# Experts with few rows multiplied in plain fp32 on the two column halves of TensorE, and a new order around gathers, pairs and splits

## The chip, the cores and the metric

The kernel runs on one core of a Trainium2 chip. The metric is the device time of one execution in microseconds (us); three executions of the kernel before took 3588.44 to 3592.20 us, with a median of 3590.94 us.

## What is computed

One layer of a streaming encoder on 1152 tokens of 2048 numbers (1024 of a prompt, 8 x 16 of running streams): a projection, a gated convolution and differential attention, an output projection, then a mixture of experts and a last norm. The change lies in the mixture of experts:

```
lg = hf @ w_rg + b_rg                       # 4 groups of experts, the best one is taken
le_g = (hf @ w_re + b_re)[that group]       # 8 experts in it, the best two are taken
xs = hf[tok_s]                              # tokens in the order of their experts
gate, up = split(ragged_dot(xs, w_ei, sizes))          # w_ei: 32 x 2048 x 1024
ys = ragged_dot(silu(gate) * up, w_eo, sizes)          # w_eo: 32 x 512 x 2048
y = zeros.at[tok_s].add(ys * w_s)
```

Everything is fp32. There are 2304 rows (two per token) over 32 experts. Counted with the reference on its own inputs, experts 0 to 31 get 93, 74, 55, 185, 49, 149, 43, 88, 22, 15, 12, 18, 13, 28, 27, 11, 44, 16, 29, 205, 118, 23, 86, 17, 68, 190, 228, 61, 34, 179, 14 and 110 rows: 19 experts have at most 64, seven have 65 to 128 (0, 1, 7, 20, 22, 24, 31), six have more (3, 5, 19, 25, 26, 29). The eleven experts 8 to 18 are all among the 19.

## The kernel before, in words

`phase_experts` (L1495) works through **groups**, each one expert with up to 256 rows, so here 32 groups, one per expert. A group has one tile of 128 rows, or two (a **pair**), and every tile costs the same however many of its rows are real. First the routing is planned: VectorE (DVE) finds for each row its place, 18 indirect transfers write a table of slots (L1653), and a small plan says for each group its expert and how many pairs lie before it (`group_expert`, `group_pairs`).

For a group, 12 **units** of 1 MB are loaded by the SP queue (`load_unit`, L1485): units 0 to 7 are pieces of `w_ei` (two blocks of 128 rows x 1024), units 8 to 11 are column blocks of `w_eo`. They land in six buffers, `expert_raw`. TensorE multiplies here in a fast format (fp32r) that rounds its operands, so each operand is used as a rounded part and a remainder: ScalarE (ACT) writes the rounded part of a unit, `e_w_hi` (`split_hi`, L1887 to L1891), DVE the remainder, `e_w_lo` (`split_lo`, L1976 to L1979), into four buffers each. The remainder's end frees the raw buffer (`lo_done`), which the next load waits for (L1600). Three products, hi by hi, lo by hi and hi by lo, then make one fp32 product (L1805 into the four PSUM banks `e_gu`, L1782 into `e_y_ps`).

The rows of a group are gathered from HBM by GpSimd's queue (L1640) into `e_x`, turned by TensorE against the identity (L1736, `turn_rows`), and kept as `e_xT_hi` by ACT (L1896) and `e_xT_lo` by DVE (L1984). After the eight units of `w_ei`, ACT computes silu (L1928), DVE multiplies by the other half (L2117), TensorE turns the result (L1769), ACT and DVE keep it as two parts (L1933, L2122), and the four units of `w_eo` follow. In between TensorE turns the next group's rows. ACT copies each output block to `e_y` (L1965), and GpSimd scatters it to `expert_rows` (L1711); the scatter's landing frees `e_y` (`y_free`).

Where the next group is a pair, its second tile is turned in a step of its own at the end of `up_and_first` of the group in front (L1852 to L1860), and kept by ACT and DVE (L1951, L2140), before that group's last three output blocks. In a pair each unit is used for both tiles before the next unit.

Each engine runs its own loop of 40 possible groups, each inside `If(g < count)` (L1566), and chooses between code for one and for two tiles (`by_size`, L1576).

Of the kernel before, what the change touches and what calls it, by code (L numbers as in the profile page):

```python
# [1481 lines left out]
UIN, UOUT = KT // 2, D // 512  # L1482

def load_unit(c, eng, raw, raw_loaded, expert, u):  # L1485

    r = u % RAW
    if u < UIN:
        w = c.io.w_ei.rearrange("e (u a p) n -> e u p a n", a=2, p=P)[ds(expert, 1), u, :, :, :].rearrange("e p a n -> (e p) a n")
    else:  # L1490
        w = c.io.w_eo.rearrange("e (k p) (b n) -> e b p k n", p=P, n=512)[ds(expert, 1), u - UIN, :, :, :].rearrange("e p k n -> (e p) k n")
    eng.dma_start(raw[:, r, :].rearrange("p (a n) -> p a n", a=w.shape[1]), w).then_inc(raw_loaded[r], 16)

def phase_experts(c, raw, raw_loaded, x_back, w_hi, w_lo, rows_back, rows_loaded):  # L1495
# [14 lines left out]
    with ExitStack() as mem:  # L1510
# [5 lines left out]
        pos, rows = sb("e_pos", [P, NP], U32), sb("e_rows", [P, NP, 4], I32)  # L1516
        empty = sb("e_empty", [P, 2 * SLOT_GROUPS, 4], I32)
# [3 lines left out]
        with ExitStack() as once:  # L1521
# [16 lines left out]
            expert_col, paired_col = first("r_expert_col", [P, 1]), first("r_paired_col", [P, 1])  # L1538
# [4 lines left out]
        sg, act_rows = sb("e_sg", [P, 2, DE]), sb("e_act", [P, 2, DE])  # L1543
# [22 lines left out]
        def groups(eng, count, body):  # L1566
# [4 lines left out]

        def pairs(eng, g):

            return eng.value_load(c.group_pairs[0:1, ds(g, 1)], min_val=0, max_val=MAXG)

        def by_size(eng, before, after, part):  # L1576

            with eng.If(before < after):
                part(2)
            with eng.If(before == after):  # L1580
                part(1)
# [12 lines left out]
        with nc.Block() as block:  # L1594

            @block.sync
            def _(sp):
# [20 lines left out]
                groups(sp, count, body)  # L1618
# [19 lines left out]
            def _(pool):  # L1638
# [4 lines left out]
                def gather(g, before, after):  # L1643
# [4 lines left out]
                    gather_tile(0)  # L1648
                    with pool.If(before < after):
                        gather_tile(1)  # L1650
# [12 lines left out]
                pool.memset(empty[:], 0).then_inc(consts, 1)  # L1663
# [7 lines left out]
                pool.memset(empty[:, :, 0:2], NO_ROW).then_inc(consts, 1)  # L1671
                pool.wait_ge(consts, 14)
                pool.dma_start(io.slots.rearrange("(p t) f -> p (t f)", p=P), empty[:].rearrange("p t f -> p (t f)")).then_inc(emptied, 16)
                pool.wait_ge(emptied, 16)
# [5 lines left out]
                p0, p1, p2 = (pairs(pool, g) for g in range(3))  # L1680
# [3 lines left out]
                gather_tile(0)  # L1684
                with pool.If(p0 < p1):
                    gather_tile(1)
# [4 lines left out]
                pool.dma_start(table[:, 2:6, :], slot_tiles[:, 2:6, :]).then_inc(next_loaded, 16)  # L1691
                pool.dma_start(table[:, 6:, :], slot_tiles[:, 6:, :]).then_inc(table_loaded, 16)
                pool.wait_ge(next_loaded, 16)
                pool.wait_ge(x_turned, 4 * p1 + 4)
                gather(1, p1, p2)

                def body(g):
                    here, nx, nx2, nx3 = (pairs(pool, g + i) for i in range(4))
                    pool.wait_ge(table_loaded, 16)
                    pool.wait_ge(x_turned, 4 * (g + nx2 + 2))  # L1700
                    gather(g + 2, nx2, nx3)
# [5 lines left out]
                    def scatter(n):  # L1707
                        pool.wait_ge(y_kept, 4 * (g + here + n) + 2)
                        c.hold(pool)
                        for r in range(n):  # L1710
# [4 lines left out]
                    by_size(pool, here, nx, scatter)  # L1715
# [3 lines left out]
                groups(pool, count, body)  # L1719
                all_pairs = pairs(pool, MAXG)  # L1720
                pool.wait_ge(y_stored, 16 * (count + all_pairs))
                pool.wait_ge(x_loaded, 16 * (count + all_pairs + 2))

            @block.tensor
            def _(pe):
# [3 lines left out]
                def turn_rows(tile, r, quads):  # L1729

                    for q in quads:
                        if q >= 2:
                            pe.wait_ge(x_kept, 4 * tile + q - 1)
                        for j in range(4):
# [5 lines left out]
                pe.wait_ge(consts, 14)  # L1740
# [3 lines left out]
                pe.wait_ge(columns_ready, 2)  # L1744
                S = SLOT_GROUPS
                pe.matmul(gu_ps[0:1, 2, 0:S], expert_col[0:S, :], c.ident[0:S, 0:S], start=True, stop=True)
                pe.matmul(gu_ps[0:1, 3, 0:S], paired_col[0:S, :], tri[0:S, 0:S], start=True, stop=True).then_inc(plan_turned, 1)
# [7 lines left out]
                count, p1 = group_count(pe), pairs(pe, 1)  # L1755
                pe.wait_ge(x_loaded, 16 * p1 + 16)
                turn_rows(0, 0, range(4))
                with pe.If(p1 > 0):
                    pe.wait_ge(x_kept, 4)
                    turn_rows(1, 1, range(4))  # L1760

                def body(g):
                    here, nx, nx2 = (pairs(pe, g + i) for i in range(3))
# [32 lines left out]
                    def up_and_first(n):  # L1796

                        tile = g + here + n
                        pe.wait_ge(x_kept, 4 * (g + here + n))
                        pe.wait_ge(a_kept, 2 * (g + here) + 1)  # L1800

# [7 lines left out]
                        PASSES = ((xT_hi, w_hi), (xT_hi, w_lo), (xT_lo, w_hi))  # L1809
                        for u in range(UIN):  # L1810
                            s = u % SPL
                            pe.wait_ge(lo_done[u % RAW], 2 * g + u // RAW + 2)
                            if u < UIN - 1:
# [17 lines left out]
                        pe.wait_ge(x_loaded, 16 * (g + nx2 + 2))  # L1831
                        turn_rows(tile, 0, (0,))
# [4 lines left out]
                        turn_rows(tile, 0, (1,))  # L1837
# [6 lines left out]
                        turn_rows(tile, 0, (2, 3))  # L1844
# [577 lines left out]
```

## Time and profile before

| | before |
|---|---|
| median of three executions | 3590.94 us |
| profiled execution, its own time | 3590.53 us |
| its span, first to last instruction | 3588.5 us |
| mean granted TensorE clock | 0.971 of 2.4 GHz |
| TensorE matmul busy | 3366.8 us, 94% |
| DVE, ACT, GpSimd busy | 1683.9, 1288.3, 1021.6 us |
| weight units of the experts loaded | 256 of w_ei, 128 of w_eo, 1024 KB each |
| DMA over the whole span | 691.62 MB, mean 193 GB/s |

The experts' stage lies between about 2105 and 3497 us of the span; the part in front of it is not touched by the change. Busy shares are means over stages with different limits; the DMA and clock figures of single stretches say more, and stand with the rows below.

### The profile page before, as it was taken

What the parts mean: (1) busy time and instruction counts of PE and PEld (TensorE: products, weight loads), DVE (VectorE), ACT (ScalarE), POOL (GpSimd) and SP (SyncE); (2) the same over time, 40 slices, a digit from 0 to 9 for tenths busy, and PEclk for the clock granted to TensorE, in tenths of its full rate; (3) what the DMA queues carried; (4) which work ended last, traced back from release to release, by engine and by line L of the source; (5) the groups of instructions that cost most, each with busy time, mean ns of one, the idle gap of its engine ahead of it and who ended that gap; (6) DMA issues with size and microseconds to landing.
All of it is one profiled execution on the core that took longest, in us unless ns stands there. A gap on an engine that the chain in (4) does not pass through costs nothing. (4 is left out here: it accounts for less than half of the span.)

```text
span 3588.5 us, 51245 instructions
## 1 busy us (share of the span) xinstructions
PE 3366.8 (94%) x18439; PEld 2950.7 (82%) x18440; DVE 1683.9 (47%) x1742; ACT 1288.3 (36%) x1577; POOL 1021.6 (28%) x761
## 2 busy tenths in 40 slices
PE   8999999999999998989999869999999999999990
PEld 8999999999999975668888657787888788778770
DVE  4222222000111147860111267658888858846677
ACT  4000000000000035750101246657787757746572
POOL 3444444444444301234445431101111101101010
PEclk9999999999999998999999879999999999999995
DMA  4121111212222391116445469679999979967688
GB/s 150 60 67 54 54 54 58 76 61 75 87 80 67 124 348 61 54 42 238 156 124 164 152 216 356 244 258 354 364 353 369 360 253 369 370 218 268 255 336 361
DMA packets 341083, 691.62 MB, mean 193 GB/s; under 512 B 23034, under 2 KB 151482, under 8 KB 330511
## 3 DMA queue, kind: packets, MB, share of 16 engines
q1 hardware_dynamic: 291508, 585.75, 45.9%
q10 hardware_dynamic: 37163, 66.14, 4.9%
q0 software_dynamic: 12336, 38.69, 3.1%
q8 instruction: 51, 0.84, 0.1%
q14 instruction: 25, 0.20, 0.0%
HBM read 637.25 MB, written 97.28 MB: 205 GB/s over the span
## 5 line engine op out<-in xcount | busy, mean ns | idle before, releaser
L1979 DVE TENSOR_TENSOR e_w_lo<-expert_raw,e_w_hi 128x2048 fp32r<-128x2048 f32 x388 | 872.8, 2288 | 255.1 <-ACT e_w_hi L1891 231.9
L1891 ACT ACTIVATE e_w_hi<-expert_raw 128x2048 fp32r<-128x2048 f32 x388 | 744.3, 1919 | 301.9 <-PE e_gu L1805 253.3
L295 PE MATMUL p_z<-hT_hi,p_w_hi 128*128 128x384 f32 x2256 | 755.3, 335 | 2.4 <-DVE p_xs L432 2.4
L297 PE MATMUL p_z<-hT_hi,p_w_lo 128*128 128x384 f32 x2256 | 753.8, 334 | 0.0
L296 PE MATMUL p_z<-hT_lo,p_w_hi 128*128 128x384 f32 x2256 | 753.7, 334 | 0.0
L295 PEld LDWEIGHTS p_z<-hT_hi,p_w_hi 128*128 128x128 f32 x2256 | 423.6, 188 | 2.7 <-DVE p_xs L432 2.7
L296 PEld LDWEIGHTS p_z<-hT_lo,p_w_hi 128*128 128x128 f32 x2256 | 423.6, 188 | 0.0
L297 PEld LDWEIGHTS p_z<-hT_hi,p_w_lo 128*128 128x128 f32 x2256 | 423.5, 188 | 0.0
L1805 PE MATMUL e_gu<-e_w_hi,e_xT_hi 128*128 128x512 f32 x1216 | 390.4, 392 | 6.6 <-issue 6.6
L1805 PE MATMUL e_gu<-e_w_lo,e_xT_hi 128*128 128x512 f32 x1216 | 387.8, 390 | 0.0
L1805 PE MATMUL e_gu<-e_w_hi,e_xT_lo 128*128 128x512 f32 x1216 | 387.8, 390 | 0.0
L277 POOL TENSOR_TENSOR p_w_raw<-p_w_raw,gain 128x1024 f32<-128x1024 f32 x96 | 182.2, 1898 | 668.8 <-issue 332.6
L1805 PEld LDWEIGHTS e_gu<-e_w_hi,e_xT_hi 128*128 128x128 f32 x1216 | 227.1, 188 | 60.7 <-issue 14.6
L1805 PEld LDWEIGHTS e_gu<-e_w_lo,e_xT_hi 128*128 128x128 f32 x1216 | 228.8, 188 | 48.1
L1805 PEld LDWEIGHTS e_gu<-e_w_hi,e_xT_lo 128*128 128x128 f32 x1216 | 228.8, 188 | 47.9
L1645 POOL COPY e_gather_idx<-e_table 128x2 int32 (+1 forms) x33 | 6.7, 204 | 879.9 <-PE e_t L1736 690.6
L283 POOL TENSOR_TENSOR p_w_lo<-p_w_raw,p_w_hi 128x1024 fp32r<-128x1024 f32 x96 | 237.7, 2476 | 7.7
L626 ACT ACTIVATE d_kT<-p_t 128x512 f32<-128x512 f32 x8 | 4.4, 596 | 613.0 <-DVE p_rows L496 602.3
L1782 PE MATMUL e_y_ps<-e_w_hi,e_aT_hi 128*128 128x512 f32 x608 | 199.9, 410 | 14.8 <-DVE e_w_lo L1979 6.9
L534 ACT ACTIVATE p_e_hi<-p_e 128x1152 fp32r<-128x1152 f32 x8 | 9.3, 1168 | 568.9 <-DVEq L476 568.9
L1429 DVE TENSOR_TENSOR m_x<-m_z,m_x 128x512 f32<-128x512 f32 x36 | 24.6, 692 | 373.1 <-PE m_z L2308 372.7
L1782 PE MATMUL e_y_ps<-e_w_lo,e_aT_hi 128*128 128x512 f32 x608 | 192.6, 398 | 0.0
(337 smaller groups left out, 4642.4 us busy)
## 6 DMA issues: line engine op xcount, KB each, us to landing
expert_raw<-w_ei SPq DMA_DIRECT2D x256, 1024.0 KB, 8.6
expert_raw<-w_eo SPq DMA_DIRECT2D x128, 1024.0 KB, 10.4
p_w_raw<-w_in SPq DMA_DIRECT2D x96, 512.0 KB, 4.0
m_w_raw<-w_out SPq DMA_DIRECT2D x64, 512.0 KB, 4.4
d_k<-cache_k SPq DMA_DIRECT2D x8, 2048.0 KB, 14.6
d_v<-cache_v SPq DMA_DIRECT2D x8, 2048.0 KB, 9.9
rows_back<-expert_rows SPq DMA_DIRECT2D x12, 1024.0 KB, 15.8
n_x<-x SPq DMA_DIRECT2D x9, 1024.0 KB, 5.9
```

The costliest lines, as they stand in the source:

```text
L277: pool.tensor_tensor(w_raw[:, part, :], w_raw[:, part, :], c.gain[:, part].unsqueeze(2).to_broadcast([P, HALF, P]), ALU.mult).then_inc(ste ...
L283: pool.tensor_tensor(w_lo[:, part, :], w_raw[:, part, :], w_hi[:, part, :], ALU.subtract).then_inc(split[half], 1)
L295: pe.matmul(out, w_hi[:, k, :], x_hi[:, xk, cols], start=(k == 0), stop=False)
L296: pe.matmul(out, w_hi[:, k, :], x_lo[:, xk, cols], start=False, stop=False)
L297: mm = pe.matmul(out, w_lo[:, k, :], x_hi[:, xk, cols], start=False, stop=(k == KT - 1))
L534: act.activation(e_hi[:], e[:], ACT.Copy).then_inc(hi_ready, 1)
L1429: dve.tensor_tensor(x[:, s, :], z[:, s, :], x[:, s, :], ALU.add).then_inc(x1_ready, 1)
L1645: pool.tensor_copy(gather_idx[:], field(g, 0)).then_inc(idx_ready, 1)
L1782: mm = pe.matmul(y_ps[:, m % 2, :], a_part[:, r, k, :], w_part[:, s, k * 512:(k + 1) * 512], start=(k == 0 and a_part is aT_hi and w_part ...
L1805: return pe.matmul(gu_ps[:, 2 * r + h, :].rearrange("p (b n) -> p b n", b=2), x_part[:, r, k, :], w[:, :, h, :], start=(k == 0 and x_part ...
L1891: act.activation(w_hi[:, s, :], raw[:, r, :], ACT.Copy).then_inc(hi_done, 1)
L1979: dve.tensor_tensor(w_lo[:, s, :], raw[:, r, :], w_hi[:, s, :], ALU.subtract).then_inc(lo_done[r], 1)
```

## The change

The plan gets a third column, `group_kind`: 1 (small) for an expert with at most 64 rows, 2 (full) for 65 to 128, 3 for a pair; group 0 is never small. Each engine chooses its code by it (`by_kind`).

```diff
+BLOCK_OF = (0, 2, 1, 3)
+FEW = P // 2
+SMALL, FULL, PAIR = 1, 2, 3
-        def by_size(eng, before, after, part):
+        def by_kind(eng, g, part):
+            kind = kind_of(eng, g)
+            for k in (SMALL, FULL, PAIR):
+                with eng.If(kind == k):
+                    part(k)
```

**A small group** isn't split. TensorE multiplies the raw units in plain fp32, with the 64 columns of `e_xT` (kept exactly by a new DVE copy, for every group's first tile) as the stationary operand, once on each half of the array's columns: the two halves take two column blocks of a unit at the same time and write partitions 0 to 63 and 64 to 127 of one bank. The raw buffer is freed by the product itself.

```diff
+                    def up_small():
...
+                        for u in range(UIN):
+                            pe.wait_ge(raw_loaded[u % RAW], 32 * g + 16 * (u // RAW) + 16)
+                            for a in range(2):
...
+                                for h in range(2):
+                                    mm = pe.matmul(bank[side(h)], xT[:, k, :], w[:, :, h, :], start=(k == 0), stop=(k == KT - 1))
...
+                            mm.then_inc(lo_done[u % RAW], 1)
+                    def out_small(i):
...
+                        for k in range(KE):
+                            for h, u in enumerate(units):
+                                mm = pe.matmul(y_ps[side(h), i, :], aT[:, k % 2, side(k // 2)], raw[:, u % RAW, k * 512:(k + 1) * 512],
+                    def group(kind):
+                        if kind == SMALL:
+                            up_small()
+                            pe.wait_ge(x_loaded, 32 * (g + 2))
+                            turn_rows(g + 1, g + here + 1, 0, (0,))
+                            turn_act_small()
+                            turn_rows(g + 1, g + here + 1, 0, (1, 2, 3))
+                            for i in range(UOUT // 2):
+                                out_small(i)
```

ACT and DVE handle both halves of a small group in one silu, one product, one copy of the turned result, and two copies to `e_y`; the scatter sends half rows by an index of its own (`twice_idx`, written once the scatter before has landed). The blocks of `w_eo` are loaded in the order 0, 2, 1, 3.

```diff
                     for q in quads:
                         dve.wait_ge(x_hi, 4 * tile + q + 1)
+                        dve.tensor_copy(xT[:, 4 * q:4 * q + 4, :], bank(t_ps, q % 2)[:, :, 0:FEW]).then_inc(x_exact, 1)
                         dve.tensor_tensor(quad(xT_lo, r, q), bank(t_ps, q % 2), quad(xT_hi, r, q), ALU.subtract).then_inc(x_kept, 1)
+                    def keep_small(split):
+                        for i in range(UOUT // 2):
+                            if split:
+                                split_hi(g + 1, i)
+                            for h in range(2):
+                                product_done(UIN + 2 * i + h)
+                            c.hold(act)
+                            act.activation(y[:, 0, i * 512:(i + 1) * 512], y_ps[:, i, :], ACT.Copy,
+                                           scale=column_twice(g, 0)).then_inc(y_kept, 2)
```

**A pair** turns its second tile at its own beginning and, while that tile is kept, multiplies its first four units for the first tile alone; these four units' second tile follows.

```diff
-                    by_size(pe, here, nx, up_and_first)
-                    with pe.If(nx < nx2):
...
+                        if n == 2:
+                            turn_second()
...
+                        for u in range(SPL if n == 2 else 0):
+                            pe.wait_ge(lo_done[u % RAW], 2 * g + u // RAW + 2)
...
+                                        product(u, a, 0, x_part, w_part, h)
+                        if n == 2:
+                            pe.wait_ge(x_kept, 4 * tile)
```

**Gathers and tables:** every group gathers two tiles (a row that isn't there is skipped), the gather of group 1 is issued in front of the large table load, and two more table loads (`e_twice`) follow it. The slots have six fields for four; four more iotas fill the new ones, and three transfers for one clear the table. DVE computes the new column in seven small steps, in front of the first gather's index. TensorE and ACT run all 40 rounds of the loop without `If(g < count)`; a round without a group falls through three comparisons.

## Rows read from the trace of the kernel before

**Rows 1.** Span of the core in us and its mean granted TensorE clock.
```profile
core 0: 3588.5 us, clock 0.971
```
**Rows 2.** Busy time by stretch: group 10 (one tile), then most of pair 19.
```profile
core 0: us, PE busy (x) PEld busy (x) DVE busy (x) ACT busy (x) POOL busy (x), PEclk, DMA share, GB/s
...
2545.00:2581.00 36.00, 35.87 (x167) 29.15 (x166) 31.42 (x21) 28.68 (x25) 4.53 (x4) 1.00 0.95 359
...
2873.00:2943.00 70.00, 69.69 (x317) 57.11 (x316) 37.40 (x27) 35.54 (x35) 4.61 (x4) 1.00 0.67 240
```
**Rows 3.** Timeline of GpSimd, scatters that end groups 0, 10, 11, 18, 19, 31: start, length.
```profile
2147.40 1.90 POOL L1711 DMA_INDIRECT expert_rows<-e_y,e_row_idx  x1 [7.76 <-ACT e_y L1965]
...
2585.36 1.93 POOL L1711 DMA_INDIRECT expert_rows<-e_y,e_row_idx  x1 [7.72 <-ACT e_y L1965]
...
2621.20 1.93 POOL L1711 DMA_INDIRECT expert_rows<-e_y,e_row_idx  x1 [7.71 <-ACT e_y L1965]
...
2877.63 1.98 POOL L1711 DMA_INDIRECT expert_rows<-e_y,e_row_idx  x1 [7.67 <-ACT e_y L1965]
...
2946.79 1.02 POOL L1711 DMA_INDIRECT expert_rows<-e_y,e_row_idx  x1 [18.12 <-ACT e_y L1965]
...
3497.30 1.93 POOL L1711 DMA_INDIRECT expert_rows<-e_y,e_row_idx  x1 [7.71 <-ACT e_y L1965]
```
**Rows 4.** Waits: engine and line, for whom: us in total, times, longest us.
```profile
ACT e_w_hi L1891 <- PE e_gu L1805: 253.3, 176, 11.4
...
ACT e_w_hi L1891 <- DMA expert_raw<-w_ei: 24.8, 20, 3.1
...
DVE e_w_lo L1979 <- issue: 23.0, 18, 1.8
...
DVE rows_back L2205 <- PEq L1594: 13.6, 1, 13.6
```
**Rows 5.** Waits of the SP queue, which issues the loads.
```profile
SPq L1492 <- DVE e_w_lo L1979: 1108.5, 378, 21.9
```
**Rows 6.** Busy time by stretch (columns as in rows 2): longest run of loads within group 7.
```profile
2446.00:2467.00 21.00, 20.87 (x102) 17.15 (x101) 17.35 (x15) 15.17 (x15) 0.18 (x1) 1.00 1.04 402
```
**Rows 7.** Timeline inside pair 3: ACT's splits of one unit and the next.
```profile
2242.13 1.92 ACT L1891 ACTIVATE e_w_hi<-expert_raw 128x2048 fp32r<-128x2048 f32 x1 [3.52 <-PE e_gu L1805]
...
2247.57 1.92 ACT L1891 ACTIVATE e_w_hi<-expert_raw 128x2048 fp32r<-128x2048 f32 x1 [3.52 <-PE e_gu L1805]
```
**Rows 8.** Timeline of TensorE, decode stage: four fp32 products on four column quarters, twice.
```profile
1293.65 1.04 PE L709 MATMUL d_s<-d_kT,d_qx 128*32 128x512 f32 x8
1294.51 0.23 PE L712 MATMUL d_s<-d_kn,d_qx 128*32 128x16 f32 x8
1294.57 1.05 PE L709 MATMUL d_s<-d_kT,d_qx 128*32 128x512 f32 x8
```
**Rows 9.** Groups by line and shape, 2150 to 3500 us: busy us, mean ns of one.
```profile
L1984 DVE TENSOR_TENSOR e_xT_lo<-e_t,e_xT_hi 128x512 fp32r<-128x512 f32 x124 | 79.9, 686 | 8.6 <-ACT e_xT_hi L1896 7.0
...
L2117 DVE SCALAR_TENSOR_TENSOR e_act<-e_gu,e_table,e_sg 128x256 f32<-128x256 f32 x74 | 35.1, 483 | 63.1 <-ACT e_sg L1928 63.1
...
L2122 DVE TENSOR_TENSOR e_aT_lo<-e_gu,e_aT_hi 128x256 fp32r<-128x256 f32 x74 | 30.3, 423 | 34.3 <-ACT e_aT_hi L1933 32.2
```
**Rows 10.** Timeline inside group 7: turned rows, DVE's run of splits, product of unit 10.
```profile
2464.28 1.04 PE L1736 MATMUL e_t<-ident,e_x 128*128 128x128 f32 x8
...
2466.75 13.32 DVE L1979 TENSOR_TENSOR e_w_lo<-expert_raw,e_w_hi 128x2048 fp32r<-128x2048 f32 x6
...
2469.35 0.62 PE L1782 MATMUL e_y_ps<-e_w_hi,e_aT_hi 128*128 128x512 f32 x2
```
**Rows 11.** DMA issues: count and median us from issue to landing.
```profile
expert_rows<-e_y,e_row_idx POOLq DMA_INDIRECT x38, 8.8
```
**Rows 12.** Busy time by stretch (columns as in rows 2): end of attention, then its beginning.
```profile
1556.00:1564.00 8.00, 5.56 (x45) 4.08 (x41) 5.29 (x10) 5.54 (x16) 2.61 (x5) 1.00 0.00 0
1348.00:1360.00 12.00, 6.32 (x51) 3.10 (x43) 2.01 (x3) 0.79 (x2) 0.57 (x4) 0.50 0.41 130
```

More of the change, by code:

```diff
@@ L1641, in gather_tile, with gather @@
                         ap=gather_idx[:, r:r + 1].bitcast(U32), axis=0), bounds_check=TOK - 1, oob_is_err=False).then_inc(x_loaded, 16)
-                def gather(g, before, after):
+                def gather(g):
                     c.hold(pool)
@@ L1647, in gather @@
                     c.hold(pool)
-                    gather_tile(0)
-                    with pool.If(before < after):
-                        gather_tile(1)
+                    for r in range(2):
+                        gather_tile(r)
                 def scatter_slots(n):
@@ L1670, in _ @@
                                    channel_multiplier=-1).then_inc(consts, 1)
[L1671 to L1674, printed above, removed]
+                pool.wait_ge(consts, 13)
+                for third in range(3):
+                    pool.dma_start(io.slots.rearrange("(p t) f -> p (t f)", p=P)[:, third * empty.shape[1]:(third + 1) * empty.shape[1]],
+                                   empty[:]).then_inc(emptied, 16)
+                for k in range(TOPK):
+                    for h in range(2):
+                        pool.iota(rows[:, k * NT:(k + 1) * NT, 4 + h], pattern=[[2 * P, NT]], base=2 * k * TOK + h, channel_multiplier=2).then_inc(consts, 1)
+                pool.wait_ge(consts, 17)
+                pool.wait_ge(emptied, 48)
                 pool.wait_ge(slots_ready, 1)
@@ L1679, in _ @@
                 count = group_count(pool)
-                p0, p1, p2 = (pairs(pool, g) for g in range(3))
+                p1 = pairs(pool, 1)
                 pool.wait_ge(x_cleared, 2)
@@ L1727, in _, with turn_rows @@
                 pe.sem_inc(y_kept, 2)
-                def turn_rows(tile, r, quads):
+                def turn_rows(g, tile, r, quads):
                     for q in quads:
@@ L1754, in _ @@
                 pe.wait_ge(plan_ready, 1)
[L1755 to L1760, printed above, removed]
+                pe.wait_ge(x_loaded, 32)
+                turn_rows(0, 0, 0, range(4))
                 def body(g):
-                    here, nx, nx2 = (pairs(pe, g + i) for i in range(3))
+                    here = pairs(pe, g)
                     def turn_act(r, h):
```

270 lines of the change are left out of this document (191 added, 79 removed).

## The prediction

> **What bounds the kernel now.** I began with the span: the profiled execution took 3590.53 us, of which 3588.5 are span [rows 1] and 2.0 lie around it; the median of three is 3590.94, so a sum made against 3590.5 holds for it too. A measurement of this kernel can tell about 0.2%, some 7 us, from no change.
>
> The stretches come next. In a group of one tile TensorE is busy 35.87 of 36 us at the full clock while the DMA engines move 359 GB/s at a busy share of 0.95; in a pair TensorE is busy 69.69 of 70 us at 240 GB/s [rows 2]. So TensorE sets the pace, but in the groups of one tile the transfers are close behind it. The scatters, one step per group, give the prices [rows 3]. A group of one tile takes 2621.20 - 2585.36 = 35.84 us, for 12 rows as for 118. A pair takes 2946.79 - 2877.63 = 69.16. From the first scatter to the last are 1349.90 us in 31 steps: 25 x 35.84 + 6 x 69.16 = 1311.0, and the 38.9 left are 6.5 for each of six pairs, the step in which a pair's second tile is turned during the group in front.
>
> The waits say the same: ACT's splits wait 253.3 us for TensorE's products and 24.8 for loads of `w_ei` [rows 4]; the SP queue has 1108.5 us of waiting for a raw buffer [rows 5]. Where it needn't wait the transfers are faster: 402 GB/s over 21 us at a share of 1.04 [rows 6]. This is the ceiling I use. A one-tile group moves 35.84 us x 359 GB/s = 12.87 MB, so it can't be shorter than 32.0 us in a row of its like, 2.67 a unit.
>
> **Small groups: TensorE's price.** Split work costs 2247.57 - 2242.13 = 5.44 us a unit in a pair, 2.72 for one tile [rows 7]. The new product on column halves isn't in this kernel, but its neighbour is: four plain fp32 products of 512 columns, each on a quarter of the array, are eight instructions, and the next instruction begins 1294.51 - 1293.65 = 0.86 us later [rows 8] (the 1.04 us in the row reach to the modelled end of the last). So four of them take no longer than one must: they run together. For two on halves 0.86 is the floor, and twice that the ceiling, if they take turns. I take 0.86, since this row is the nearest there is: 16 row blocks of `w_ei` make 13.8 us, four row blocks for each of two pairs of `w_eo` units 6.9.
>
> Between them lies a chain. DVE's product takes 0.48, and I give ACT's silu of the same shape as much; the copy of the turned result about 0.42 [rows 9], the two turns of it some 0.4; then the next rows' third and fourth quads wait for two exact copies (0.42 each by the same row) and two remainders of 0.69. With some 0.2 us at each of six handovers this is 5.5 us, in which the 16 turns (eight in 1.04 us, [rows 10]) are hidden. With 0.8 for handovers at the ends, a small group is 27.0 us of TensorE's order; 25.5 to 30 are its bounds.
>
> New waits there: DVE stands at the head of a small group until the scatter before has landed, 8.8 us after its issue [rows 11], some 11 after that group's products. Behind it are only the product after silu, needed 14 us in, so it costs nothing; if a pair's two scatters are 3 us later it costs one or two.
>
> **Which small groups get 27.** A full group or a pair leaves six loaded units behind it. The small group that follows runs at 27.0; there are eight such (2, 4, 6, 8, 21, 23, 27, 30): 8 x 8.84 = 71 us. The second in a row (9 and 28) finds about two units and ends when ten more have come and the last two are multiplied, 10 x 2.67 + 3.4 = 30.1: 2 x 5.7 = 11. The other nine (10 to 18) run at the transfers' pace of 32.0: 9 x 3.84 = 35. Together 117. The chain in the middle doesn't stop the transfers: with TensorE waiting for loads all six buffers are on order, 16 us of them, when it comes.
>
> **Pairs.** The 6.5 us in front of each go. TensorE pays 2.1 for the 16 turns [rows 10]; keeping them, and the wait for that, lie beside four units of one tile, 10.9 us; DVE's exact copies add some 0.4. So 4.0 each, 24; two pairs (19 and 29) follow small groups that run at the transfers' pace and wait one us for their first split: 22. If that cover were gone the old price would be back.
>
> **Full groups** get dearer. DVE has four more copies, 1.7 us by the nearest row (0.42), before its run of splits. That run has no room: six splits take 13.32 us, so unit 10's remainder, the first, ends at 2466.75 + 2.22 = 2468.97, and its product begins at 2469.35 [rows 10]. So some 1.4 us of the 1.7 reach TensorE, seven times: 10 us against. The floor is 0, the ceiling 1.7 each.
>
> **Plan, gathers, tables, loops.** Seven steps and one copy on DVE stand before the first gather, and the first turn now waits for a second gather that brings nothing; neither is in this trace. The steps work on fewer numbers than the 0.48 us product [rows 9], so eight are at most 3.9 us; a scatter's issue takes 1.9 [rows 3] and I allow the gather as much. Between 0 and 6 us; I take the middle, 3. Iotas and clearing wait for nothing new. The large table load now stands in GpSimd's queue behind the gather of group 1 and two more table loads, but what waits for it on DVE and ACT stands at the end of group 0. In GpSimd's queue the scatter stands behind a gather that waits for a pair's turns, now a few us later; `e_y` isn't needed until far into that pair. The double gathers, and the SP queue's loads in another order, cost GpSimd and SP time that nobody waits for. Register loads and comparisons: 23.0 us over 18 waits now, 1.3 each [rows 4], in the shadow of queued products; full groups pay already above. The eight empty rounds have three comparisons for one; DVE waits 13.6 us for the block's end after its last split [rows 4], which covers most. I take 1 us, 0 to 6.
>
> **Sum.** 117 + 22 - 10 - 3 - 1 = 125; 3590.5 - 125 = 3465.
>
> **Rivals.** *The loads have a lower ceiling.* The 359 GB/s of every group of one tile could be what the weights get over a whole group, the 402 only a stretch of it. Then a small group in a row costs 35.8, the nine gain nothing (-35), groups 9 and 28 take 33 (-6), the four full groups behind a small one (7, 22, 24, 31) wait 2.5 each (-10) and first small groups lose 6: 125 - 57 = 68, so 3522. Against it speaks that SP was waiting for buffers and TensorE was busy all the while. The Trainium skill, page "HBM Reference", section "Specifications (TRN2)", states about 358 GB/s effective per core, which would make this rival the forecast; it adds that a core streaming alone measures about 425, and the 402 here agree with the second.
>
> *TensorE falls to its lower level in small groups.* It now waits for loads, and in the trace it has 1.2 GHz where it was busy 6.32 of 12 us (clock 0.50), but 2.4 GHz where it was busy 5.56 of 8 (1.00) [rows 12]. A small group has 23 of 32 us of work, about the second. If the lower level held, the products would cost 41.4 for 20.7 and the group 47.7; 19 x 11.9 = 226 lost, so 3800. It decides against the change where the mean small group is over 35.84 + (22 - 10 - 4) / 19 = 36.3 us, that is with 45% of the products at the lower level. But at 47.7 TensorE would have no waits left, which speaks against its staying there.
>
> *The change doesn't do what it says:* the halves take turns, on the same bank and the same stationary rows. The products cost 41.4 again: 3800. The rows speak against it, but with quarters [rows 8].
>
> **How the numbers follow.** Forecast 0.84, lower ceiling 0.08, lower clock 0.04, halves in turn 0.04. Within the forecast: eight small groups at 25.5 or 30 (-12 or +24), the transfers 10 GB/s faster or slower than 402 over eleven groups (0.8 us each, 9 either way), full groups at 0 (-10), start and end at their bounds (-4, +8). Not all at once: 3435 to 3510; outside it are the rivals and little else. Faster by more than 0.2%: 0.91, counting both ways of being faster and leaving 0.01 for a draw; slower 0.08.
>
> **What would show it.** Right: scatters of groups 10 to 18 about 32 us apart at over 395 GB/s, first small groups about 27, pairs about 72 with no long step in front, full groups about 37. ACT's and DVE's splits fall by 19 x 12 = 228 of 388. Wrong: small groups at 36 with a DMA share near 1 (first rival); PEclk near 0.5 there (second); pairs of half products 1.7 us apart (third); or a gap of more than 7 us between silu and the first product of `w_eo`.

## The result and the profile after

The changed kernel takes 3549.26 us (median of four, 3542.64 to 3549.82), the kernel before on the same chip 3591.57 (four, 3588.44 to 3594.24): the ratio is 0.9878, 95% interval 0.9861 to 0.9895. It is faster by 42 us, where 125 were forecast, and lies outside the range. The profiled execution of it is its fastest one, 3542.64, so the account below is of 3590.53 - 3542.64 = 47.9 us.

The core's span and clock, of the changed kernel [rows 1]:

```profile
core 0: 3541.0 us, clock 0.960
```

Busy time by stretch (columns as in [rows 2]): groups 10 to 17, all small; small group 8, behind a full one; small group 4, behind a pair; full group 7, behind a small one; pair 19.

```profile
2531.20:2800.10 268.90, 210.03 (x914) 68.42 (x912) 40.55 (x96) 33.10 (x56) 27.39 (x40) 0.96 1.01 388
...
2470.40:2497.90 27.50, 24.01 (x116) 8.79 (x117) 5.01 (x12) 4.14 (x7) 3.43 (x5) 1.00 0.96 350
...
2294.50:2328.10 33.60, 28.52 (x132) 11.28 (x131) 7.71 (x14) 8.23 (x10) 2.00 (x2) 0.90 0.90 331
...
2429.80:2470.40 40.60, 39.07 (x164) 31.04 (x164) 30.64 (x23) 26.22 (x23) 6.43 (x5) 0.92 0.98 380
...
2839.20:2908.40 69.20, 68.82 (x312) 56.68 (x313) 41.58 (x34) 37.06 (x38) 12.67 (x9) 1.00 0.73 267
```

The bound has changed sides. In group 10 of before TensorE was busy 35.87 of 36 us [rows 2]; in the row of small groups it is busy 210 of 269, and the DMA engines nearly all the time (a share of 1.01; 1.03 to 1.05 is the most that the rows here show, since packets overlap a little). Eight groups in 268.90 us are 33.6 each, where 32.0 were forecast. Group 8, whose loads lay ready, took the 27.5 that was TensorE's price. DVE and ACT are out of the matter: 41 and 33 us of 269, where they had 31 and 29 of 36.

GpSimd's timeline says the same with the scatters that end groups 0, 9, 17 and 31 [rows 3]:

```profile
2156.64 1.04 POOL L1751 DMA_INDIRECT expert_rows<-e_y,e_row_idx  x1 [2.18 <-issue]
...
2533.23 1.03 POOL L1746 DMA_INDIRECT expert_rows<-e_y,e_twice_idx  x1 [5.87 <-issue]
...
2802.18 1.03 POOL L1746 DMA_INDIRECT expert_rows<-e_y,e_twice_idx  x1 [6.21 <-issue]
...
3449.11 2.04 POOL L1751 DMA_INDIRECT expert_rows<-e_y,e_row_idx  x1 [5.43 <-ACT e_y L2070]
```

The steps from the first scatter to the last shrank from 1349.9 to 1292.5 us, by 57.4; but the first scatter comes 9.2 us later. That is group 0, and it is the second thing to explain.

The waits, 2100 to 3450 us (engine and line, for whom: us, times, longest), show what TensorE waits for now. Waits of PE and of PEld overlap.

```profile
PEld e_gu L1937 <- DMA expert_raw<-w_ei: 152.9, 90, 4.4
...
PE e_gu L1937 <- DMA expert_raw<-w_ei: 75.4, 79, 3.5
ACT e_w_hi L1999 <- DMA expert_raw<-w_ei: 70.3, 37, 6.5
...
POOL e_gather_idx L1670 <- DMA e_table<-slots: 17.3, 2, 15.6
```

ACT's waits for loads rose from 24.8 us [rows 4] to 70.3, and TensorE now waits for loads itself, at L1937, the products of small groups.

The steps, each from the first product of `w_ei` in a group to the first one of the next group (TensorE's timeline; for the small groups behind a pair up to the end of their own products), with three of the experiments below:

| us | before | forecast | after | half_loads | no_rows | wide_rows |
|---|---|---|---|---|---|---|
| small groups 10 to 17, mean | 35.9 | 32.0 | 33.6 | 27.3 | 31.6 | 32.0 |
| small group 8, behind a full one | 36.8 | 27.0 | 27.5 | 26.9 | 25.8 | 26.1 |
| small groups behind a pair (4, 6, 27, 30), mean | | 27.0 | 30.4 | 27.3 | 27.4 | 27.2 |
| full groups 7, 22 and 31, behind a small one, mean | 35.9 | 37.2 | 40.1 | 37.1 | 38.9 | 40.2 |
| group 0 | 40.1 | 41.5 | 48.3 | 53.5 | 44.7 | 48.0 |
| pair 19 | 69.2 | 69.6 | 69.2 | 69.2 | 69.2 | 69.3 |

The last step, of group 31, ends with its last product. By kind, before and after: the 19 small groups took 706.8 us and take 633.8 (-73.0, with what four pairs behind them saved), the seven full ones 261.0 and 290.2 (+29.3), the six pairs 422.3 and 417.3 (-5.0). Sum -48.7; the start is 0.5 later and the end costs 0.3 more.

Set against the forecast's terms, step by step, some 75 of the 77 us that are missing can be placed: 31 in the eight small groups that were to run at 27.0 us (their steps hold the wait for the next group's first split), 17 in the nine that were to take 32.0, 10 in groups 9 and 28, 15 in the four full groups behind a small one and 7 in group 0; the rest comes to 4 or 5 the other way. The row of groups 10 to 17 is the cleanest place to ask why, not the largest part.

### The profile page after: what moved, and what is told of

Its sections match the earlier page's. It is cut to its first block and busy times, and to the rows that moved or that the text cites. A ratio compares the mean times of both kernels' runs of the same rounds, so it can differ in the third digit from the quotient of the medians.

```text
span 3541.0 us, 48577 instructions
## 1 busy us (share of the span) xinstructions
PE 3188.3 (90%) x17491; PEld 2570.3 (73%) x17492; DVE 1209.1 (34%) x1654; ACT 827.5 (23%) x1254; POOL 1032.1 (29%) x796
## 5 line engine op out<-in xcount | busy, mean ns | idle before, releaser
L2127 DVE TENSOR_TENSOR e_w_lo<-expert_raw,e_w_hi 128x2048 fp32r<-128x2048 f32 x160 | 363.8, 2289 | 205.3 <-ACT e_w_hi L1999 203.8
L1999 ACT ACTIVATE e_w_hi<-expert_raw 128x2048 fp32r<-128x2048 f32 x160 | 306.3, 1916 | 234.1 <-PE e_gu L1846 153.6
L1937 PE MATMUL e_gu<-expert_raw,e_xT 128*64 128x512 f32 x1216 | 290.0, 612 | 75.6 <-DMA expert_raw<-w_ei 75.4
L1937 PEld LDWEIGHTS e_gu<-expert_raw,e_xT 128*64 128x64 f32 x1216 | 80.7, 138 | 277.2 <-DMA expert_raw<-w_ei 152.9
L1846 PE MATMUL e_gu<-e_w_hi,e_xT_hi 128*128 128x512 f32 x608 | 201.0, 402 | 25.9 <-DVE e_w_lo L2127 16.6
L1846 PE MATMUL e_gu<-e_w_lo,e_xT_hi 128*128 128x512 f32 x608 | 198.6, 399 | 0.0
L1846 PE MATMUL e_gu<-e_w_hi,e_xT_lo 128*128 128x512 f32 x608 | 198.4, 398 | 0.0
L1846 PEld LDWEIGHTS e_gu<-e_w_hi,e_xT_hi 128*128 128x128 f32 x608 | 116.8, 194 | 55.7 <-DVE e_w_lo L2127 21.6
L2477 POOL TENSOR_TENSOR m_w_lo<-m_w_raw,m_w_hi 128x1024 fp32r<-128x1024 f32 x64 | 155.8, 2434 | 5.0
L1959 PE MATMUL e_y_ps<-expert_raw,e_aT 128*64 128x512 f32 x608 | 144.7, 624 | 5.4 <-DMA expert_raw<-w_eo 5.4
```

The source lines that it names most:

```text
L1846: return pe.matmul(gu_ps[:, 2 * r + h, :].rearrange("p (b n) -> p b n", b=2), x_part[:, r, k, :], w[:, :, h, :], start=(k == 0 and x_part ...
L1937: mm = pe.matmul(bank[side(h)], xT[:, k, :], w[:, :, h, :], start=(k == 0), stop=(k == KT - 1))
L1959: mm = pe.matmul(y_ps[side(h), i, :], aT[:, k % 2, side(k // 2)], raw[:, u % RAW, k * 512:(k + 1) * 512], start=(k == 0), stop=(k == KE - 1))
L1999: act.activation(w_hi[:, s, :], raw[:, r, :], ACT.Copy).then_inc(hi_done, 1)
L2127: dve.tensor_tensor(w_lo[:, s, :], raw[:, r, :], w_hi[:, s, :], ALU.subtract).then_inc(lo_done[r], 1)
L2477: pool.tensor_tensor(self.lo[:, s], self.raw[:, s], self.hi[:, s], ALU.subtract).then_inc(self.split_done, 1)
```

## The experiments

Two questions were open: is the shortfall in the loads or in TensorE's own order, and if in the loads, which part of them.

**half_loads.** All loads of the loop fetch half of their bytes.

```diff
-    eng.dma_start(raw[:, r, :].rearrange("p (a n) -> p a n", a=w.shape[1]), w).then_inc(raw_loaded[r], 16)
+    a = w.shape[1] // part
+    eng.dma_start(raw[:, r, 0:D // part].rearrange("p (a n) -> p a n", a=a), w[:, 0:a, :]).then_inc(raw_loaded[r], 16)
```

> The loads of weights that follow the first six bring half of their bytes (the other half of a buffer keeps what it had), so this kernel leaves out part of the weights; all instructions of TensorE, ACT and DVE stay. Theory A, the shortfall is in the loads: then every small group runs at the 27.5 us of the one that had its loads (group 8), 19 of them in 522 us and 8 for the turns of four pairs behind them, where they took 634 us; the full groups behind a small one fall from 40 to 37 us. 634 - 530 = 104, and 16: about 3430 us. Rival B, TensorE's own order (the chain in the middle, its lower clock after idling) is dearer than was counted: small groups stay at 30 us or more, about 3480 or above.

3419.32 us in one run, against 3430 expected. Busy time of groups 10 to 17:

```profile
2509.40:2727.60 218.20, 200.18 (x914) 73.17 (x912) 40.83 (x96) 33.06 (x56) 27.45 (x40) 0.94 0.71 247
```

The same 914 instructions on TensorE, 27.3 us a group, at a clock of 0.94. So TensorE's price was right (27.0 forecast), the halves of the array run together, and the shortfall is in the transfers. The granted clock is lower here than in the changed kernel (0.94 and 0.96), so the clock isn't what made that one long.

**no_small.** Is it the small groups at all? The planner calls none small.

```diff
-then(dve.tensor_scalar(full_slots[:], group_no[:], 1.0, float(FEW), ALU.min, ALU.mult))
+then(dve.tensor_scalar(full_slots[:], group_no[:], 1.0, 0.0, ALU.min, ALU.mult))
```

> The planner calls no group small: a used group is full or a pair, and everything else of the change stays; nothing is left out. By the terms of the forecast: 3591 - 24 for the pairs (4.0 for each of six) + 25 full groups at 0.5 (as group 20 shows) to 1.4 each + 8 for the table wait + 1: 3588 to 3611. If the pairs gain less than was counted (the prep step goes on in another place), 3600 to 3630; the steps in front of and of pairs tell it: 35.8 + 2.1 + 69.2 + 0.4 expected for the two.

3595.02 us, ratio 1.001 (1.000 to 1.002), as expected. Scatters of two groups in a row:

```profile
2593.12 2.05 POOL L1751 DMA_INDIRECT expert_rows<-e_y,e_row_idx  x1 [5.42 <-ACT e_y L2070]
2629.38 2.04 POOL L1751 DMA_INDIRECT expert_rows<-e_y,e_row_idx  x1 [5.43 <-ACT e_y L2070]
```

A full group takes 36.26 us where it took 35.84 [rows 3]: the extra copies on DVE cost 0.4, not 1.4. The six steps in front of pairs fell by 15.5 us together (43.4 to 40.7, 39.5 to 37.9, 41.1 to 39.5, 40.9 to 38.3, 76.5 to 70.8, 43.0 to 41.7), and groups 0 and 1 rose by 12. So the gain of the change comes from the small groups, and the loss in group 0 is there without them.

**turns_behind.** Group 11 and its like begin `w_eo` 3 us after its rows are ready, since the turns of the third and fourth quad stand in front. Does that hold the buffers so long that the loads pause?

```diff
-turn_rows(g + 1, g + here + 1, 0, (1, 2, 3))
-for i in range(UOUT // 2):
-    out_small(i)
+turn_rows(g + 1, g + here + 1, 0, (1,))
+out_small(0)
+turn_rows(g + 1, g + here + 1, 0, (2, 3))
+out_small(1)
```

> In small groups the turns of the third and fourth quad of the next rows stand behind the first product of w_eo instead of in front of it; nothing is left out. Theory A1: between the last product of w_ei and the end of the first pair of w_eo products no buffer comes free, 9.9 us, and the six loads on order last less than that, so that the transfers stop for some 1.5 us in every small group. The product of w_eo stands ready 3.0 us earlier than it begins; begun then, the stretch is 6.9 us, the dip in the transfers goes, groups 10 to 17 fall from 33.6 to 32.2 us (+-0.4), small groups that had loads to spare by up to 3: 3549 - 8 x 1.4 - 11 x 2 to 3 = 3505 to 3520. Rival A2: 383 GB/s is simply what the weights get in such a row; groups 10 to 17 stay at 33.6 and the time is 3535 to 3549.

3553.79 us, ratio 0.9895 (0.9878 to 0.9911). Groups 10 to 17:

```profile
2537.30:2807.20 269.90, 203.55 (x914) 68.37 (x912) 40.07 (x96) 32.23 (x56) 27.44 (x40) 0.98 1.02 386
```

33.7 a group at 386 GB/s, where the changed kernel had 388: A1's 32.2 did not come. That refutes only the reordering, not the pause: the first product then waited for the second unit of its pair, and the SP queue's longest wait for a buffer in this row is 7.9 us where it was 9.1. rows_units, below, mends that, and no_rows comes back to the pause.

**few_products.** The other end of the same question: take half of the `w_ei` products away.

```diff
-                            for a in range(2):
+                            for a in range(1, 2):
```

> In small groups TensorE leaves out the products of every other row block of w_ei, so that it needs some 20 us for a group instead of 27.3; loads and all else stay. Here the transfers alone set the pace of small groups in a row. Theory A: a unit of w_ei lands 2.56 us after the one before, one of w_eo 2.71, 31.3 a group, and gather and scatter cost some 0.9: groups 10 to 17 take 32.2 (31.8 to 32.6), as the forecast had it; the 1.4 us above it in the changed kernel come from buffers that are held too long. Rival C, the ceiling over a whole group is 383 GB/s: they stay at 33.4 to 33.8.

3543.53 us in one run. Groups 10 to 17:

```profile
2535.50:2803.90 268.40, 189.74 (x660) 55.23 (x660) 40.36 (x96) 33.69 (x56) 27.35 (x40) 0.77 1.01 389
```

33.5 us with 660 instructions instead of 914, and with a mean clock of 0.77. A's 32.2 was wrong, C's number right. Neither the number of products nor the clock matters to this row: the transfers alone set it, at 389 GB/s. The question became why 389, when [rows 6] had 402.

**rows_units.** Where the trace has only one kind of load in flight, the rate differs. In the changed kernel, `w_eo` alone (2 KB in a row) and then `w_ei` alone (4 KB):

```profile
2549.00:2555.00 6.00, 3.58 (x20) 1.54 (x18) 1.80 (x5) 1.57 (x3) 0.00 (x0) 1.00 1.05 387
2539.00:2543.00 4.00, 2.82 (x12) 0.83 (x14) 0.30 (x2) 0.00 (x0) 0.00 (x0) 1.00 1.02 413
```

Here a small group's `w_eo` is loaded by row blocks (8 KB in a row), each unit serving both halves of the array; the turns stand as in turns_behind, and a buffer also comes free sooner.

```diff
+    elif small:
+        w = c.io.w_eo.rearrange("e (k p) (a n) -> e k p a n", p=P, a=1)[ds(expert, 1), u - UIN, :, :, :].rearrange("e p a n -> (e p) a n")
...
+for k in (2 * i, 2 * i + 1):
+    u = UIN + k
+    pe.wait_ge(raw_loaded[u % RAW], 32 * g + 16 * (u // RAW) + 16)
+    for n in range(2):
+        for h in range(2):
+            b = 2 * h + n
+            mm = pe.matmul(y_ps[side(h), n, :], aT[:, k % 2, side(k // 2)], raw[:, u % RAW, b * 512:(b + 1) * 512],
+                           start=(k == 0), stop=(k == KE - 1))
```

> The turns stand as in turns_behind, and a small group's four units of w_eo are whole row blocks (8 KB a row) instead of column blocks: the first product needs one unit landed, not two, and each buffer comes free after 2 us of products instead of two after 4; nothing is left out. Theory A1 as mended: in turns_behind the first product waited for the second unit of its pair (landed 5.4 us after the last unit of w_ei), so the stretch without a free buffer was still 9 us. Here it is some 5, the transfers go on, and groups 10 to 17 fall to 32.2 us (+-0.4); small groups with loads to spare to 26: 3549 - 8 x 1.3 - 6 to 15 = 3523 to 3533. Rival C: groups 10 to 17 at 33.4 or more, the time at 3543 to 3553.

3533.79 us, ratio 0.9837 (0.9815 to 0.9858). Groups 10 to 17, and a stretch in which `w_eo` alone moves:

```profile
2536.80:2797.90 261.10, 206.95 (x913) 64.70 (x913) 40.07 (x96) 31.35 (x56) 27.43 (x40) 0.97 1.01 400
...
2583.00:2589.00 6.00, 4.27 (x18) 1.17 (x20) 0.00 (x0) 0.00 (x0) 0.00 (x0) 1.00 1.02 420
```

32.6 a group. The number came, but the run has two reasons in it: `w_eo` moves at 420 GB/s instead of 387, and buffers come free sooner. The first is worth four units of 1.05 MB at 2.50 instead of 2.71 us, 0.8 of the 1.0 us gained. The second is small but not nothing, though the share is 1.01 before and after. In most groups of the changed kernel's row the transfers dip for 1 to 2.5 us, while the SP queue waits for buffers that the products of `w_eo` hold; here in group 10, and the queue's waits in the whole row:

```profile
2561.00:2563.50 2.50, 2.50 (x14) 0.84 (x12) 0.00 (x0) 0.69 (x1) 0.04 (x1) 1.00 0.67 192
...
SPq L1496 <- PE e_y_ps L1959: 88.6, 16, 9.1
```

Added up over the packets of the trace (each one short of sixteen in flight counted as an idle engine), the engines' mean idle time in groups 10 to 17 is 5.6 us in the changed kernel (0.7 a group), 4.4 in turns_behind and 2.6 in rows_units, so a shorter pause is worth up to 0.4 us a group of this gain.

**wide_rows.** rows_units with the same lever on the other weights too, and no change to when buffers come free: neighbouring rows of `w_ei` go to one partition (8 KB in a row).

```diff
-w = c.io.w_ei.rearrange("e (u a p) n -> e u p a n", a=2, p=P)
+w = c.io.w_ei.rearrange("e (u p a) n -> e u p a n", a=2, p=P)
...
-x[:, r, k * P:(k + 1) * P]
+x[:, r, (k // 2) * 2 * P + k % 2:(k // 2 + 1) * 2 * P:2]
```

> rows_units, with w_ei loaded so that each partition takes two neighbouring rows (8 KB in one piece) where it took two rows 128 apart (4 KB each); TensorE turns every other column of the rows to match; nothing is left out. Theory W, the engines' price per KB falls with the length of the piece (44.0 ns at 2 KB, 39.8 at 4, 39.0 at 8), and that, not a pause, sets the row of small groups: a unit of w_ei lands 2.49 us after the one before instead of 2.55, groups 10 to 17 fall from 32.4 to 31.9 us, the time by 5 to 10 to 3524 to 3530. Rival: the pace is that of the whole stretch (HBM), 32.4 and 3534 stay.

3520.24 us, ratio 0.9807 (0.9791 to 0.9824): the fastest version here, 1.9% under the kernel before and 29 us under the changed one. TensorE's timeline, where its products of `w_ei` wait for loads, first in the changed kernel, then in this one:

```profile
2544.68 1.94 PE L1937 MATMUL e_gu<-expert_raw,e_xT 128*64 128x512 f32 x8 [0.62 <-DMA expert_raw<-w_ei]
2547.24 1.94 PE L1937 MATMUL e_gu<-expert_raw,e_xT 128*64 128x512 f32 x8 [0.62 <-DMA expert_raw<-w_ei]
```

```profile
2575.28 1.94 PE L1945 MATMUL e_gu<-expert_raw,e_xT 128*64 128x512 f32 x8 [0.55 <-DMA expert_raw<-w_ei]
2577.76 1.94 PE L1945 MATMUL e_gu<-expert_raw,e_xT 128*64 128x512 f32 x8 [0.55 <-DMA expert_raw<-w_ei]
```

A unit every 2.56 us there, every 2.48 here; between them the eight products of a unit, two row blocks on two halves, take their 1.94. Groups 10 to 17 of wide_rows:

```profile
2527.10:2783.20 256.10, 205.37 (x912) 66.87 (x912) 40.08 (x96) 32.06 (x56) 27.39 (x41) 0.99 1.01 408
```

32.0 a group, 31.9 expected: theory W holds (the total lies 4 us below the range expected). Of the 13.6 us under rows_units some 8 are a stall in front of pair 3 that this kernel doesn't have (below, at group 0).

**no_rows.** In the changed kernel eight units of `w_ei` at 2.56 us and four of `w_eo` at 2.71 are 31.3, and the group takes 33.6. What takes the rest? From group 2 on `bound` is 0 here, so that gathers and scatters let nothing but row 0 through: the moving of rows is left out.

```diff
-axis=0), bounds_check=TOK - 1, oob_is_err=False).then_inc(x_loaded, 16)
+axis=0), bounds_check=bound, oob_is_err=False).then_inc(x_loaded, 16)
...
-bounds_check=2 * TOPK * TOK - 1, oob_is_err=False).then_inc(y_stored, 16)
+bounds_check=0, oob_is_err=False).then_inc(y_stored, 16)
...
-bounds_check=TOPK * TOK - 1, oob_is_err=False).then_inc(y_stored, 16)
+bounds_check=0, oob_is_err=False).then_inc(y_stored, 16)
```

> From group 2 on the gathers bring no rows and the scatters write none (their bounds let nothing but row 0 through; the output rows are filled beforehand with other data, which lengthens the time ahead of group 0); loads of weights, products and waits stay. So the moving of rows is left out. Theory R: in groups 10 to 17 the loads land every 2.56 us (w_ei) and 2.71 us (w_eo), 31.3 a group, and the other 2.0 to 2.3 of the 33.5 are what gather and scatter take of the DMA engines: 31.3 (31.0 to 31.8) here; small groups behind a pair (4, 6, 27, 30), beside whose first loads the pair's two scatters run, fall by 2 to 4 us each to 27 to 29 with nothing counted behind them. Rival: the 2 us are a pause of the loads (full buffers) and the wait behind a pair is the restart of the loads: 33.3 stays, and groups 4, 6, 27, 30 fall by less than 1.

3507.39 us in one run, with group 0 beginning 31.6 us later than in the changed kernel (2137.7 for 2106.1) for the filling. Groups 10 to 17, and group 4, behind a pair:

```profile
2549.70:2802.10 252.40, 205.11 (x914) 69.25 (x912) 40.29 (x96) 33.11 (x56) 27.44 (x40) 0.97 1.04 399
2327.40:2356.30 28.90, 26.93 (x132) 11.01 (x131) 7.59 (x14) 8.03 (x10) 2.02 (x2) 0.94 0.90 331
```

31.6 a group, and the small groups behind a pair fall from 30.4 to 27.4, TensorE's price. Theory R's numbers came in both places. The 2.0 us of the row are of two kinds, though: the engines' time for the rows' packets (8.9 us less over the eight groups, 1.1 a group) and the dip of rows_units (0.7 a group in the changed kernel, none here). The SP queue still waits as long for its buffers, so the pause alone makes no dip in the transfers; it needs the rows beside it:

```profile
SPq L1496 <- PE e_y_ps L1964: 84.1, 15, 9.2
```

How the rows bring it about, no run shows. Groups 2 to 31 together take 1193 us where they took 1254. What was taken out is 33 MB, which GpSimd's queue moves in that stretch of the changed kernel beside 379 MB of weights:

```profile
q1 hardware_dynamic: 128194, 378.82, 79.9%
q0 software_dynamic: 13845, 33.03, 7.0%
```

**warm.** Full groups behind small ones take 40 us, and TensorE has the lower clock (0.50, 1.2 GHz) at their head, behind a wait of 3 to 3.6 us. Is it the clock?

```diff
+with pe.If(kind_of(pe, g + 1) != SMALL):
+    for j in range(8):
+        pe.matmul(gu_ps[:, 3, 0:2 * P].rearrange("p (a b) -> p a b", a=2), c.ident[:], aT[:], start=True, stop=True)
```

> At the end of a small group that a full group or a pair follows, TensorE multiplies eight times the turned rows with the identity into a bank that nobody reads, some 2 to 3 us in the 3.0 to 3.6 us in which it waits for the first split; nothing is left out. In the changed kernel it runs at the lower clock for 6.8 us at the head of such a full group (7, 22, 24). Theory K, the lower clock makes these groups dear: they keep the full clock and the products of w_ei take 22 us where they took 24.9 to 26.3; the groups 7, 22, 24 fall by 2 to 3 us each. Rival L, they are dear because they go at the pace of the loads: full clock or not, the group takes 40 to 46 us as before (within 1 us).

3561.05 us in one run; the extra products lengthen the wait in front of pairs 3, 5, 19 and 29, where there was less to fill, by 2.2 to 3.5 us each. Group 22 with its first 6 us, in the changed kernel and here:

```profile
2976.00:2982.00 6.00, 6.00 (x14) 4.74 (x15) 4.56 (x2) 5.26 (x4) 1.62 (x1) 0.50 1.03 410
...
2976.00:3016.40 40.40, 39.09 (x166) 31.09 (x166) 30.64 (x23) 26.37 (x23) 6.43 (x5) 0.92 1.00 384
```

```profile
2993.20:2999.00 5.80, 5.80 (x27) 4.80 (x26) 5.16 (x3) 4.46 (x4) 1.61 (x1) 1.00 1.02 409
...
2993.20:3033.60 40.40, 37.42 (x168) 30.24 (x166) 30.66 (x23) 25.29 (x23) 6.80 (x5) 0.96 1.00 387
```

The products of `w_ei` then took 22.1 us instead of 24.9, and the rest of the group 18.3 instead of 15.5: 40.4 both times, with the DMA share at 1.00. Groups 7 and 24 took 42.3 and 45.1 where they had taken 40.6 and 46.5. K fell, L holds, with a spread of 1.7 us instead of 1.

**tables_first** and **table_later.** Group 0 grew from 40.1 to 48.3 us, and ACT and DVE wait for the large table at its end. Two ways to take that wait away: load the tables earlier, or wait for them later.

```diff
+for h in range(2):
+    pool.dma_start(twice[...]).then_inc(twice_loaded, 16)
+pool.dma_start(table[:, 6:, :], slot_tiles[:, 6:, 0:4]).then_inc(table_loaded, 16)
 pool.wait_ge(next_loaded, 16)
 pool.wait_ge(x_turned, 4 * p1 + 4)
 gather(1)
-for h in range(2):
-    pool.dma_start(twice[...]).then_inc(twice_loaded, 16)
-pool.dma_start(table[:, 6:, :], slot_tiles[:, 6:, 0:4]).then_inc(table_loaded, 16)
```

> The large table load and the two loads of the doubled table are issued in front of GpSimd's wait for the first turns and of the second gather, instead of behind it; nothing is left out. Theory: group 0 ends with 7.2 us in which ACT and DVE wait for that table, and they go: group 0 from 48.3 to 40.5 us, the total by 7 to 10 to about 3541. Rival: the wait only moves (the first loads of group 1 or the gather of group 2 end last): 3546 to 3549.

3558.34 us, ratio 0.9903 (0.9886 to 0.992): dearer, in a third way that neither side had. TensorE's timeline in group 0:

```profile
2145.02 1.11 PE L1777 MATMUL e_t<-ident,e_x 128*128 128x128 f32 x4 [11.66 <-DMA e_x<-xg,e_gather_idx]
...
2167.32 1.22 PE L1846 MATMUL e_gu<-e_w_hi,e_xT_hi 128*128 128x512 f32 x2 [5.57 <-issue]
```

The gather is now issued behind the table loads and lands 14.4 us later, so TensorE waits 11.7 us for its rows; and the wait at the end of the group is there all the same, 5.6 us, though the large table had landed at 2140.1.

For table_later, ACT's code (DVE's is the same):

```diff
-act.wait_ge(table_loaded, 16)
-act.wait_ge(twice_loaded, 32)
+with act.If(g != 0):
+    act.wait_ge(table_loaded, 16)
+    act.wait_ge(twice_loaded, 32)
```

> ACT and DVE wait for the large table and for the doubled one only from group 1's end on (a small group waits for the doubled one at its head), not at group 0's; nothing is left out and nothing is loaded in another order. Theory: the table lands 17 to 19 us after its issue, behind the gather, and the 5.6 to 7.2 us at the end of group 0 go: 3541 to 3544 where it was 3549. Rival: the first product of group 1 then waits for the rows of the gather or for splits: 3547 to 3550.

3549.14 us, ratio 0.9884 (0.9863 to 0.9906), where the changed kernel has 3549.26: nothing gained. The waits for the table are gone and TensorE's wait is not, only shorter by 2.4 us, so the table was not its main cause. The first product of group 1, in the changed kernel and then in table_later:

```profile
2154.31 1.22 PE L1846 MATMUL e_gu<-e_w_hi,e_xT_hi 128*128 128x512 f32 x2 [7.19 <-issue]
```

```profile
2152.66 1.21 PE L1846 MATMUL e_gu<-e_w_hi,e_xT_hi 128*128 128x512 f32 x2 [4.75 <-issue]
```

"issue" is time in which the engine waits for nothing that the profile shows. What the profile of the DMAs does show in this stretch of the changed kernel (2146 to 2156 us) is code:

```profile
q8 instruction: 3, 0.05, 3.4%
```

Three pieces of 16 KB, the first two begun at 2147.2, as the wait begins, and in by 2149.9; TensorE goes on at 2154.3, and what it does in the 4.4 us between the profile doesn't show. The body has three branches now, and the first way back to its head crosses code that was never run. In rows_units and in table_later the wait at group 0's end is shorter (3.7 and 4.8 us), and a second one stands at group 2's end, in front of the first pair, again with two pieces of 16 KB begun within 1.5 us of its start. In rows_units:

```profile
2228.82 1.97 PE L1918 MATMUL e_t<-ident,e_x 128*128 128x128 f32 x8 [8.28 <-issue]
```

That second wait is most of why table_later's profiled execution (3549.80 us) is longer than the changed kernel's (3542.64): its group 0 took 1.5 us less, its group 2 7.1 more. Whether the changed kernel's other three executions (3548.81 to 3549.82) have such a second wait, no trace shows. No run took this stall away, so that code is its cause is read from traces, not tried.

**best.** rows_units and table_later together.

> rows_units and table_later together; nothing is left out. If both theories hold, the gains add: 3515 to 3528. If only the table's does: 3536 to 3545.

3534.82 us, ratio 0.984 (0.9819 to 0.9861): rows_units' time, so only the first of the two gains is there, as table_later had shown.

## Why the prediction was wrong, step by step

**TensorE's price of a small group: right.** 27.0 forecast, 27.3 measured with the loads out of the way, 27.5 in group 8. The step from the four quarters of [rows 8] to two halves held, and so did the chain of 5.5 us (4.9 to 5.4 between the last product of `w_ei` and the first of `w_eo`; the terms named for it add up to 5.2). ACT's and DVE's splits fell by the 228 that were forecast, from 384 to 156 each.

**Which small groups get it: here the sum failed.** "A one-tile group moves 12.87 MB, so it can't be shorter than 32.0 us", with 402 GB/s from [rows 6], and "the small group that follows runs at 27.0". Four things were wrong in it, the first of them the step itself: a floor was taken as the price.
- The 402 came from the best 21 us of a group, and "can't be shorter than 32.0" says what no group goes under, not what it takes. The price of a load goes by its kind: 413 GB/s for `w_ei`, 387 for `w_eo`, by the same engines at a share over 1; that alone gives 31.3 for the weights, and it isn't where the time went.
- The rows had no term of their own. In [rows 2] they ride along in 359 GB/s, and a group of 12 rows was taken for all. They are 33 MB in the stage; while TensorE was the bound they cost nothing that the steps show, and once the transfers are the bound they lengthen the stage. Without them groups 10 to 17 lose 2.0 us each, and those behind a pair 3.0, because a pair's two scatters run just beside the first loads that the small group asks for. All of groups 2 to 31: 61 us, though that run idles 4.8 us in front of pair 3 (idle that ends with "issue", as in rows_units). So 61 to 66 of the 77 us that are missing go with the moving of rows.
- "The chain in the middle doesn't stop the transfers": it doesn't stop them, but with two units left on order and rows beside them they fall to 192 GB/s for 2.5 us in group 10. The idle time of the engines is 0.7 us a group, a part of the 2.0.
- The six loaded units are a loan. What a small group saves by them, the next group has to wait for: the gap in front of a full group behind a small one is 3.0 to 3.6 us, and the group then goes at the pace of its loads. The forecast let it take 37.2; it took 40.1. Even without rows it takes 38.9.

**Full groups: right in kind, too dear.** 1.4 us for the copies was forecast, 0.4 measured. **Pairs:** 4.0 each was forecast, 15.5 us for the six measured without small groups, 2.6 each. The start cost 0.5 where 3 were taken, the loop's end 0.3 where 1 was.

**The table: costed at nothing, and rightly, but group 0 was not.** The forecast had nothing for a wait of TensorE that isn't for a semaphore: 7.2 us at the end of group 0, and group 1 then takes 38.9 us where it took 36.4.

**The rivals.** The lower ceiling of the loads named the right resource and a wrong size: 3522, with small groups in a row at 35.8, where they take 33.6. It got 0.08 because SP was seen to wait for buffers; that tells that the loads weren't the bound then, not how far away they were as the bound. The rule it stood beside, some 358 GB/s for a core (the Trainium skill, "HBM Reference", "Specifications (TRN2)"), isn't this row's limit: wide_rows has 408 over eight whole groups. The lower clock appears (0.96 over groups 10 to 17, 0.92 in group 7) and costs next to nothing, since it falls in waits: few_products had 0.77 and the same time. That the halves take turns is refuted.

## What to carry to other kernels

When a change takes the engine's work away, make the budget of the next resource for whole groups of every kind and over everything that uses it: here most of the missing gain went with gathers and scatters, invisible before. The ceiling is to be taken from stretches with one kind of transfer each, not from the best mixed one, and a floor got from it is not yet the price; with the transfers as the bound, longer pieces in a row were worth more here than the reordering of TensorE that was tried.

## What wasn't expected of the hardware

At a DMA share over 1 in every case, loads of 2 KB pieces moved at 387 GB/s, of 4 KB at 413, of 8 KB at 420. The price of the pieces showed in the time of a group of the row (33.6, 32.6, 32.0 us) as one load after the other was made of longer ones; in the first of the two steps up to 0.4 us are the shorter pause.

A DMA share of 1.01 over eight groups hid dips like the one to 0.67 in group 10.

In each of these kernels TensorE stands in this stage for 3.8 to 14 us in waits of over 1.5 us that end with "issue", all in groups 0 to 2, so at the first passes over the loop's branches. The kernel before has one of 6.55 us, in front of the first product of group 0.
